# Every second pair of gate and up tiles of the gated layers made by seven products of quarter blocks

## The reference, cut to what matters

```python
def swiglu(x, w_in, w_out):
    gate, up = jnp.split(x @ w_in, 2, axis=-1)     # w_in: 1024 x 5632
    return (jax.nn.silu(gate) * up) @ w_out        # w_out: 2816 x 1024
h = h + 0.5 * swiglu(rmsnorm(h, ffn1_norm), ffn1_w_in, ffn1_w_out)   # and ffn2 after the mixer
```

## Time and profile before

| what | value |
|---|---|
| median of three runs | 2323.24 us |
| the profiled execution: its own time | 2322.17 us |
| the profiled execution: its span | 2320.4 us |
| TensorE busy | 2283.2 us, 98% of the span |
| VectorE, ScalarE, GpSimd busy | 1155.9, 913.2, 1149.5 us |
| TensorE's granted clock, mean of the span | 0.994 |
| moved by DMA | 200.09 MB, mean 86 GB/s |

### The profile page before, as it was taken

One profiled execution on the slowest core, in us unless ns is written; L12 is line 12 of the kernel. 1 busy time (PEld: TensorE's weight loads), 2 busy tenths in 40 slices (PEclk: granted clock), 3 DMA queues, 4 the chain that ended last, 5 costly groups with the idle time before them and its releaser, 6 DMA issues.

```text
span 2320.4 us, 36943 instructions
## 1 busy us (share of the span) xinstructions
PE 2283.2 (98%) x13952; PEld 1889.1 (81%) x13952; DVE 1155.9 (50%) x1772; ACT 913.2 (39%) x1456; POOL 1149.5 (50%) x687
## 2 busy tenths in 40 slices
PE   8999999999999999999999999999999989999998
PEld 7888887889988888877777778888888878888887
DVE  5442146268743431377545466614626986731732
ACT  5332225467753321255644274212234535222222
POOL 5444444544465554444555354444445973544442
PEclk9999999999999999999999999999999989999999
DMA  4232233320033322331111113223222232332231
GB/s 167 99 99 92 99 99 102 122 69 1 10 100 100 98 93 98 98 120 64 47 34 53 43 56 104 93 97 99 93 97 84 92 100 82 100 99 99 91 99 55
DMA packets 56126, 200.09 MB, mean 86 GB/s; under 512 B 6224, under 2 KB 6480, under 8 KB 56016
## 3 DMA queue, kind: packets, MB, share of 16 engines
q1 hardware_dynamic: 54432, 195.82, 25.7%
q10 hardware_dynamic: 1584, 2.75, 0.4%
HBM read 196.45 MB, written 2.10 MB: 86 GB/s over the span
## 4 chain that ended last, share of the span: by engine, by line
PE 44%; POOL 4%; issue 3%; DVE 2%; ACT 1%; POOLq 0%; DVEq 0%; ACTq 0%
PE ps L133 13%; PE ps L135 13%; PE ps L134 13%; POOL sb_w_lo L114 2%; POOL sb_caway L3060 1%; PE ps L647 1%; PE ps L2068 0%; DVE ps L3111 0%; PE ps L661 0%; POOL sb_cu_lo L3072 0%; POOL sb_cout L3066 0%; PE ps L2064 0%; PE ps L2115 0%; PE ps L2044 0%; PE ps L2013 0%
## 5 line engine op out<-in xcount | busy, mean ns | idle before, releaser
L114 POOL TENSOR_TENSOR sb_w_lo<-sb_w_raw,sb_w_hi 128x1024 fp32r<-128x1024 f32 (+1 forms) x361 | 887.1, 2460 | 929.9 <-ACT sb_w_hi L101 928.4
L133 PE MATMUL ps<-sb_xn_hi,sb_w_hi 128*128 128x512 f32 x1688 | 669.5, 397 | 6.2 <-POOL sb_w_lo L114 3.2
L134 PE MATMUL ps<-sb_xn_lo,sb_w_hi 128*128 128x512 f32 x1688 | 657.9, 390 | 0.0
L135 PE MATMUL ps<-sb_xn_hi,sb_w_lo 128*128 128x512 f32 x1688 | 657.9, 390 | 0.0
L101 ACT ACTIVATE sb_w_hi<-sb_w_raw 128x1024 fp32r<-128x1024 f32 x362 | 379.8, 1055 | 484.1 <-PE ps L135 458.1
L133 PEld LDWEIGHTS ps<-sb_xn_hi,sb_w_hi 128*128 128x128 f32 x1688 | 316.6, 188 | 78.5 <-POOL sb_w_lo L114 4.0
L135 PEld LDWEIGHTS ps<-sb_xn_hi,sb_w_lo 128*128 128x128 f32 x1688 | 316.5, 188 | 67.2
L134 PEld LDWEIGHTS ps<-sb_xn_lo,sb_w_hi 128*128 128x128 f32 x1688 | 316.6, 188 | 65.9 <-issue 2.2
L133 PE MATMUL ps<-sb_hid_hi,sb_w_hi 128*128 128x512 f32 x864 | 336.4, 389 | 2.0 <-DVE sb_hid_lo L401 2.0
L135 PE MATMUL ps<-sb_hid_hi,sb_w_lo 128*128 128x512 f32 x864 | 336.1, 389 | 0.0
L134 PE MATMUL ps<-sb_hid_lo,sb_w_hi 128*128 128x512 f32 x864 | 336.1, 389 | 0.0
(11 more groups left out here) (491 smaller groups left out, 2957.1 us busy)
## 6 DMA issues: line engine op xcount, KB each, us to landing
sb_w_raw<-weights SPq DMA_DIRECT2D x365, 512.0 KB, 3.4
sb_stage<-x SPq DMA_DIRECT2D x4, 512.0 KB, 4.7
out<-sb_out_stage SPq DMA_DIRECT2D x8, 256.0 KB, 2.9
sb_abias<-table ACTq DMA_DIRECT2D x4, 256.0 KB, 5.4
sb_lora_w<-lora ACTq DMA_DIRECT2D x2, 256.0 KB, 2.8
sb_rstd<-table ACTq DMA_DIRECT2D x1, 256.0 KB, 2.7
...
```

Source lines behind the costliest of these rows:

```text
L114: pool.tensor_tensor(c.w_lo[:, slot, 0:width], c.w_raw[:, slot, 0:width], c.w_hi[:, slot, 0:width].bitcast(F32), ALU.subtract).then_inc(c. ...
L133: pe.matmul(out, hi, rhs_hi(k0 + k), start=first, stop=False)
L134: pe.matmul(out, hi, rhs_lo(k0 + k), start=False, stop=False)
L135: mm = pe.matmul(out, lo, rhs_hi(k0 + k), start=False, stop=last)
```

## The change: what it does

A pair of gate and up tiles is a product of a weight matrix of 2x2 quarters (gate or up tile, first or second half of the inputs) with an activation matrix of 2x2 quarters (halves of the inputs, halves of the tokens). In a *folded* pair the eight products of quarters become seven (Strassen's scheme in Winograd's form). A quarter product is 4 blocks times 3 matmuls of 256 columns, so a folded pair has 84 matmuls of 256 columns where a plain one has 48 of 512. In `upA` the pairs 2, 4, ..., 14 are folded (7), in `upB` the pairs 1, 3, 5 (3); in two layers that is 20 of 44 pairs. The squared-ReLU layers keep their code.

- Four weight sums S1 to S4 per folded pair: VectorE forms them from `w_raw` (`block_sum`), ScalarE makes their hi parts (`block_high`), VectorE their lo parts (`block_low`). They and the pair's other quarters lie in half-unit places of the rings; `up_plan` writes down beforehand which place each takes and what must be over before. GpSimd makes the lo parts of the unsummed quarters, for the first unit only after all four sums are there (`fold_low`).
- Four activation sums t1 to t4, once per layer at the start of `upA` (`fold_x_dve`, `fold_x_act`): seven VectorE instructions and two ScalarE copies for each of four k.
- The seven products lie in four PSUM banks; one ScalarE copy (`fold_copy`) and six VectorE additions (`fold_adds`) join them. `hid_hi` is made by ScalarE instead of VectorE.
- The loops of the gated up phases become straight-line code, `gate` lies in `y`, and some semaphores are reused (`LOADED`). GpSimd's `rwkv_constants` are issued between pairs of `ffn2_upA` at the same pace as before.

```diff
+FOLDED = {name: range(2 if name[-1] == "A" else 1, units // 2, 2) for name, units in UP_PHASES[:4]}
+def folded(p):                                  # in fold_up_pe
+    pe.wait_ge(c.s_lo, p.u + 1)
+    pe.wait_ge(c.s_evac, p.u + START - 2)
+    block_products(pe, c, p1, p.first.spots[0], *x_part(0, 0), True, True).then_inc(c.s_used, 1)
+    block_products(pe, c, p2, p.first.spots[1], *x_part(HALF_K, 0), True, True).then_inc(c.s_used, 1)
...
+    pe.wait_ge(c.s_block_lo, p.low["S2"])
+    block_products(pe, c, p6, p.spot["S2"], *t_part(2), True, True).then_inc(c.s_used, 1)
...
+    pe.wait_ge(c.s_lo, p.u + 2)
+    block_products(pe, c, p4, p.spot["A22"], *t_part(3), True, True).then_inc(c.s_pe, 2)
+def fold_x_dve(dve, c, phase, gain, i):
...
+    for k in range(HALF_K):
...
+        dve.tensor_scalar(product, c.x[:, k], gain(k), None, ALU.mult).then_inc(c.s_sums, 1)
+        dve.wait_ge(c.s_sums, done + 1)
...
+        dve.tensor_tensor(t1, product[:, HALF_T:], product[:, 0:HALF_T], ALU.subtract).then_inc(c.s_sums, 1)
+        dve.scalar_tensor_tensor(out=t3, in0=other[:, HALF_T:], scalar=g, in1=product[:, HALF_T:], op0=ALU.mult,
+                                 op1=ALU.subtract).then_inc(c.s_sums, 1)
+        dve.wait_ge(c.s_sums, done + 2)
+        dve.scalar_tensor_tensor(out=t2, in0=other[:, HALF_T:], scalar=g, in1=t1, op0=ALU.mult,
+                                 op1=ALU.subtract).then_inc(c.s_sums, 1)
+        dve.wait_ge(c.s_sums, done + 4)
+        dve.scalar_tensor_tensor(out=t4, in0=other[:, 0:HALF_T], scalar=g, in1=t2, op0=ALU.mult,
+                                 op1=ALU.subtract).then_inc(c.s_sums, 1)
+        for x, source in enumerate((c.rstd, c.ss)):
...
+            dve.wait_ge(c.s_block_hi, t.high + 2 * k + x + 1)
+            dve.tensor_tensor(c.t_lo[:, 2 * x:2 * x + 2, k], halves(source[:]),
+                              c.t_hi[:, 2 * x:2 * x + 2, k].bitcast(F32), ALU.subtract).then_inc(c.s_block_lo, 1)
+def block_sum(dve, c, p, block):
...
+        dve.tensor_tensor(s1, a21, a22, ALU.add).then_inc(c.s_sums, 1)          # S1
...
+        dve.tensor_tensor(s2, s1, a11, ALU.subtract).then_inc(c.s_sums, 1)      # S2, waits for S1
...
+        dve.tensor_tensor(s3, a11, a21, ALU.subtract).then_inc(c.s_sums, 1)     # S3
...
+        dve.wait_ge(c.s_block_lo, p.low["S1"])
+        dve.tensor_tensor(s4, a12, s2, ALU.subtract).then_inc(c.s_sums, 1)      # S4
+def fold_up_act(act, c, phase, gated, hid_base, i):
...
+    for j, p in enumerate(pairs):
+        after = pairs[j + 1] if j + 1 < len(pairs) else None
+        if p.folded:
+            block_high(act, c, p, "A22")
+        if j > 0:
+            parts(pairs[j - 1])                 # hid_hi of the pair before
+        if p.folded:
+            fold_copy(act, c, phase, p)
+        unit_high(act, c, after.first if after is not None else phase.following[0])
+        if after is not None and after.folded:
+            block_high(act, c, after, "S2")
+            block_high(act, c, after, "S1")
+        else:
+            unit_high(act, c, after.second if after is not None else phase.following[1])
+        if j == 0 and phase.prepared:
+            fold_x_act(act, c, phase, i)
+        activations(p)                          # Silu
+        if after is not None and after.folded:
+            block_high(act, c, after, "S3")
+            block_high(act, c, after, "S4")
+def fold_up_dve(dve, c, phase, gated, hid_base, gain, i):
...
+    for j, p in enumerate(pairs):
+        after = pairs[j + 1] if j + 1 < len(pairs) and pairs[j + 1].folded else None
+        if j > 0:
+            hidden(pairs[j - 1])
+        if j > 0:
+            low(pairs[j - 1])                   # hid_lo of the pair before
+        if j == 0 and phase.prepared:
+            fold_x_dve(dve, c, phase, gain, i)
+        if after is not None:
+            block_sum(dve, c, after, "S1")
+            block_sum(dve, c, after, "S2")
+            block_sum(dve, c, after, "S3")
+        if p.folded:
+            fold_adds(dve, c, p, 0)             # 2 additions of 256 columns
+        if after is not None:
+            block_low(dve, c, after, "S2")
+            block_low(dve, c, after, "S1")
+            block_sum(dve, c, after, "S4")
+        if p.folded:
+            fold_adds(dve, c, p, 1)             # 3 additions of 256 columns
+            fold_adds(dve, c, p, 2)             # 1 addition of 512, after the pair's last product
+        if gated:
...
+            dve.tensor_tensor(gate, gate, shaped(p, c.rs[:]), ALU.mult).then_inc(c.s_gated, 1)
+        if after is not None:
+            block_low(dve, c, after, "S3")
+            block_low(dve, c, after, "S4")
+def fold_low(pool, c, phase, between=None):
...
+            if after.folded:
+                pool.wait_ge(c.s_sums, after.sums + 4)
+            unit_low(pool, c, after.first)
```

More of the change, by code:

```diff
@@ L31 @@
 SCRATCH = 2048
+LOADED = 16
 TILE_LINE = 4 * T
@@ L80, in stream_load @@
+UP_PLAN = up_plan()
 def stream_load(sp, c):
@@ L345, in renorm_dve, with wait_free, unit_high @@
                              op0=ALU.mult, op1=ALU.mult).then_inc(c.s_xr, 1)
+def wait_free(act, c, free):
+    for kind, value in free:
+        if kind == "pe":
+            act.wait_ge(c.s_pe, value + START + 1)
+        else:
+            act.wait_ge(c.s_used, value)
+def unit_high(act, c, x):
+    if x.written:
+        return
+    act.wait_ge(c.s_raw[x.u % RING], x.u // RING * 16 + 16)
+    wait_free(act, c, x.free)
+    act.activation(c.hi_blocks[:, x.spots[0]:x.spots[1] + 1].rearrange("p b k n -> p (b k) n"), c.w_raw[:, x.u % RING],
+                   ACT.Copy).then_inc(c.s_hi, 1)
@@ new lines, in unit_low, with block_products @@
+def unit_low(pool, c, x):
+    both = slice(x.spots[0], x.spots[1] + 1)
+    pool.wait_ge(c.s_hi, x.u + 1)
+    pool.tensor_tensor(c.lo_blocks[:, both].rearrange("p b k n -> p (b k) n"), c.w_raw[:, x.u % RING],
+                       c.hi_blocks[:, both].rearrange("p b k n -> p (b k) n").bitcast(F32),
+                       ALU.subtract).then_inc(c.s_lo, 1)
+def block_products(pe, c, out, spot, rhs_hi, rhs_lo, start, stop):
+    for k in range(HALF_K):
+        hi, lo = c.hi_blocks[:, spot, k], c.lo_blocks[:, spot, k]
+        pe.matmul(out, hi, rhs_hi(k), start=start and k == 0, stop=False)
+        pe.matmul(out, hi, rhs_lo(k), start=False, stop=False)
+        mm = pe.matmul(out, lo, rhs_hi(k), start=False, stop=stop and k == HALF_K - 1)
+    return mm
@@ new lines, in products_of, with fold_copy @@
+def products_of(c, p):
+    banks = folded_banks(p.j)
+    half = lambda x: (c.ps[:, banks[x], 0:HALF_T], c.ps[:, banks[x], HALF_T:])
+    (p2, p6), (p4, p3), (p7, p5), (p1, _) = (half(x) for x in range(4))
+    return p1, (p2, p6), (p5, p7), (p3, p4)
+def fold_copy(act, c, phase, p):
+    p1, _, _, _ = products_of(c, p)
+    act.wait_ge(c.s_used, p.used["A11"])
+    act.wait_ge(c.s_block_lo, phase.t.low + 2 * HALF_K)
+    act.wait_ge(c.s_add, p.add)
+    act.activation(c.ss[:, 0:HALF_T], p1, ACT.Copy).then_inc(c.s_copied, 1)
@@ new lines, in result, with shaped, parts, activations @@
+def result(c, phase, p, half):
+    if not p.folded:
+        return c.ps[:, plain_banks(phase.base, p.j)[half]]
+    banks = folded_banks(p.j)
+    in_halves = c.ps[:].rearrange("p b (h n) -> p (b h) n", h=2)
+    first, second = ((2 * banks[0], 2 * banks[1] + 1), (2 * banks[1], 2 * banks[2] + 1))[half]
+    return in_halves[:, first:second + 1:second - first]
+def shaped(p, ap):
+    return halves(ap) if p.folded else ap
+def fold_up_act(act, c, phase, gated, hid_base, i):
+    pairs = phase.pairs
+    per = 1 if gated else 2
+    def parts(p):
+        for f in range(per * p.j, per * p.j + per):
+            act.wait_ge(c.s_evac, p.u + START + (2 if gated else 1 + f % 2))
+            act.activation(c.hid_hi[:, f], c.h[:, f % 2], ACT.Copy).then_inc(c.s_hhi, 1)
+    def activations(p):
+        if gated:
+            act.wait_ge(c.s_gated, hid_base + p.j + 1)
+            act.activation(shaped(p, c.gate[:, p.j % 2]), result(c, phase, p, 0), ACT.Silu).then_inc(c.s_act, 1)
+        else:
+            for half in range(2):
+                act.wait_ge(c.s_pe, p.u + half + START + 1)
+                if p.folded:
+                    act.wait_ge(c.s_add, p.add + 6)
+                act.wait_ge(c.s_evac, p.u + half + START - 1)
+                act.activation(shaped(p, c.gate[:, half]), result(c, phase, p, half), ACT.Relu).then_inc(c.s_act, 1)
+    for j, p in enumerate(pairs):
[10 more added lines that the diff above has]
+            block_high(act, c, after, "S1")
+        else:
+            unit_high(act, c, after.second if after is not None else phase.following[1])
[5 more added lines that the diff above has]
+            block_high(act, c, after, "S4")
+    unit_high(act, c, phase.following[2])
+    parts(pairs[-1])
@@ new lines, in fold_low @@
+def fold_low(pool, c, phase, between=None):
+    pairs = phase.pairs
+    if phase.base > 0:
```

(32 more changed lines are left out.)

325 lines of the change are left out of this document (289 added, 36 removed).

## The result

The changed kernel takes 2358.72 us (median of 4 runs, 2357.84 to 2358.97), the kernel before 2322.31 (4 runs, 2321.20 to 2323.85): a ratio of 1.0155, 95% interval 1.0142 to 1.0168. The change costs 36.4 us; predicted were 2359 and a range of 2338 to 2382. The profiled executions differ by as much: spans of 2356.9 and 2320.4.

What follows compares the result with a forecast made beforehand. The prediction took TensorE, busy 98% of the span, as the bound. Its terms, -17.6 + 32.2 + 3.4 + 14.4 + 4.2 = +36.6 us on 2322.2, gave 2358.8; it said 2359, range 2338 to 2382.

Steps and rivals of the forecast that it cites:

- the 1.1 that it names: Last step of the sum: the median of the runs lies 1.1 us above the profiled execution.
- twenty folds: TensorE in the gated up phases: each folded pair takes 10.00 us instead of 10.88, twenty save 17.6 us.
- activation sums, two stalls: Before each gated layer's first folded pair, TensorE waits for VectorE's activation sums: 15.8 and 16.4 us, together 32.2.
- clock behind them: After the two long stalls TensorE runs partly at 1.2 GHz: 1.7 us lost each, 3.4 together.
- steady chain, sixteen rounds: From one folded pair over a plain one to the next, TensorE waits 0.9 us for GpSimd: 14.4 in all.
- starts of downB: After upB's folded last pair, downB's first unit gets its place late: 1.4 and 2.8 us more, 4.2 together.
- the expected wait for GpSimd: Second layer's activation sums: GpSimd's lo part, running to 680.92, holds up the first product after `rs` at 679.45.
- Rival 1: The steady chain fits beside the plain pair, so its 14.4 us go: 2344 us; chance 0.17.
- rival 2: Heavy collisions: sums in the steady chain meet GpSimd once a round, 1.1 us more sixteen times: 2376; chance 0.12.
- Rival 3: Weight loads bind in long matmul runs: 129.5 ns a matmul, so folds save nothing: 2376 us; chance 0.06.
- Rival 4: Activation sums hide beside pairs 0 and 1, removing both stalls and their clock loss: 2309 us, faster; chance 0.03.

Runs made afterwards that it cites:

- Experiments 3: The changed kernel with pair 2 of each upA left plain (folds from pair 4), all activation sums still at pair 0: 2351.76 us.
- 4: The changed kernel with upA folds from pair 4 and activation sums spread: k = 0 at pair 0, 1 at pair 1, 2 and 3 at pair 2: 2344.64 us.
- 8: The changed kernel with upA folds at 6, 8, ..., 14 and the activation sums one k at each of pairs 0 to 3: 2332.11 us.
- experiment 10: The kernel of 9 (own line) with upA folds at 5, 7, ..., 15 instead of 6, 8, ..., 14: 2324.17 us.
- experiments 7: The kernel before, with matmuls of 84 gated up units cut in two of 256 columns, no sums: 2348.94 us.
- 9: The kernel of 8 (own line), also with S1 and S2 made early, between a folded pair's last additions, and upB folding only pairs 1 and 3: 2318.23 us.

## Why the prediction was right

The sum, +36.6 us, was met to 0.1 (36.5 between the profiled spans), and the median to 0.3 us. That closeness is luck: no term is right to 0.2 us. The costs that were too high (stalls, chain, starts of downB) are 9.1 us too high, and the saving that was too high, the clock and the wait that was left out make 9.7 the other way. The last step of the sum is not right either: 2358.8 and the 1.1 that it names are 2359.9, not 2359. What was right for its own reason is that the change loses, in the places named and by the chains named. By its steps, in us, with what the traces of before and after show (distances between starts of the same matmuls):

| term | predicted | measured |
| --- | --- | --- |
| twenty folds | -17.6 | -14.2 (18 of 10.18, two of 10.07, for 10.88) |
| activation sums, two stalls | +32.2 | +28.4, and 0.8 for `rs` |
| clock behind them | +3.4 | +4.1 |
| steady chain, sixteen rounds | +14.4 | +8.6 (0.53 to 0.55 each) |
| starts of downB | +4.2 | +3.9 (2.22 and 3.66, less 1.00 twice) |
| start of the second layer's first down phase | none | +3.9, and 1.7 of clock |

They come to 37.2. Half clock in the first pair, which the trace of before happens not to have, adds about 1, and the first matmul starts 0.6 later (13.46 in place of 12.86); the unchanged parts between the layers and behind them are 2.2 shorter. That is 36.6 for the 36.5.

**The stalls.** The mechanism stood as described: 28 instructions from 27.89 to 42.6, then the chain to 52.86 (52.4 predicted). The stall is shorter than 15.8 since pair 1 began 2.3 us later (27.91 for 25.57): its matmuls now use banks that hold the norm's sum and wait 0.78 for `rs`, and the rest is the start and the clock named above. In the second layer the expected wait for GpSimd did not come about: the first product started at 695.09, when GpSimd's lo part ended, and took 0.49. Experiments 3, 4 and 8 show both halves of it: make the first fold later and the stall stands at the next plain pair; divide the block over four pairs, with two plain ones between it and the first fold, and it goes to 0.24 and 1.08 us. Over three pairs with one between it was 7.5, over four with one between (experiment 10) 4.2 and 5.1.

**The fold.** 119.9 ns a step, where 119 was predicted; but in each folded pair that waited the second matmul starts 0.23 us behind the first (141.70 to 141.93) and not 0.12, which makes 10.18. Without waits a fold is 10.08 (experiments 7, 9).

**The steady chain.** Its order and its result were right, its length 0.35 too long. Rival 1 is out, for a round is 21.60 and a shorter chain gives 20.98; rival 2 is out, for in the changed kernel none of the four sums met GpSimd. VectorE's start of S4 came at 8.20 instead of 8.43, GpSimd at 8.97 instead of 9.2, TensorE at 11.43 instead of 11.8. A sum of twelve handovers from single rows was 3% too long, and since the stall is the small remainder of a large sum, that is 40% of it.

**What was missed.** The wait at the second layer's first down phase (876.41). The prediction worked out ring places for the sums and for downB, and not for downA, where the same reasoning gives the same answer: unit 31, read to the phase's end, held the place. With its clock it is 5.6 us, and what hid it in the sum are the two terms that were too large, the chain's by 5.8 and the stalls' by 3.0.

**Rival 3** (weight load binds) is out: the 1680 matmuls of 256 columns start 120 ns apart, not 129.5. **Rival 4** (hidden activation sums) could not be: one k takes 3.64 us. The hope behind it, that the change is good when nothing waits, holds for little: 0.8 us a fold at most, 16 for twenty, against 36.5 + 14.2 = 50.7 us of waits and half clock.
